# A two-layer hybrid backbone on one core: router with stationary weights, one expert unit split by GpSimd, streamed end, later mod trips, stationary V

## What is computed

```python
# Layer l:  h = RMSNorm(x) * (1 + scale1) + shift1      (shift/scale/gate = SiLU(c) W_mod + b_mod)
#           P = h W_in  -> [q | k | v | hyena v,x1,x2 | gate_a | gate_b]
#           x += gate1 * ((sigmoid(gate_a) * A W_pa + sigmoid(gate_b) * Bh W_pb) W_o)
#           x += gate2 * FFN(RMSNorm(x) * (1 + scale2) + shift2)
def channel_mixer(h, l, ffn_w1, ffn_w3, ffn_w2, moe_router, moe_w1, moe_w3, moe_w2):
    i = l // 2
    if l % 2 == 0:
        return swiglu(h, ffn_w1[i], ffn_w3[i], ffn_w2[i])
    logits = (h @ moe_router[i]).astype(jnp.float32)
    top_val, top_idx = lax.top_k(logits, TOP_K)
    gate = jax.nn.softmax(top_val, axis=-1)
    ...
    for e in range(N_EXPERTS):
        out = out + weight[..., e:e + 1] * swiglu(h, moe_w1[i, e], moe_w3[i, e], moe_w2[i, e])
    return out
```

## Time and profile before

| | |
|---|---|
| median of 3 runs | 2063.52 us (2061.28 to 2065.64) |
| the profiled execution | 2065.47 us |
| its span in the trace | 2063.4 us |
| PE busy | 1956.9 us, 95% of the span |
| DVE busy | 1237.7 us, 60% |
| ACT busy | 999.3 us, 48% |
| GpSimd busy | 49.2 us, 2% |
| transferred | 435.46 MB, mean 211 GB/s |

### The profile page before, as it was taken

How to read it: one execution, slowest core, us unless ns; L and a number is a source line. 1 busy time by engine, 2 the same in 40 slices (tenths; PEclk the granted TensorE clock), 3 DMA queues, 4 the chain that set the end, 5 groups by cost and what they waited for, 6 DMA issues and landing times. The chain is left out here.

```text
span 2063.4 us, 24969 instructions
## 1 busy us (share of the span) xinstructions
PE 1956.9 (95%) x10036; PEld 1574.4 (76%) x10036; DVE 1237.7 (60%) x1194; ACT 999.3 (48%) x931; POOL 49.2 (2%) x57
## 2 busy tenths in 40 slices
PE   8999999998999989999998969999999999999995
PEld 3677777786888867768877967888888888888884
DVE  3444545445323322246544557897989798979894
ACT  4221145433433421134135437676777677767772
POOL 0000000002000001100000000000000000000000
PEclk9999999999999999999999969999999999999998
DMA  9641211133222246633222437897989799989991
GB/s 369 263 171 41 86 41 62 62 113 114 84 99 102 95 175 278 243 113 123 96 72 89 147 146 296 336 383 297 387 338 387 290 382 350 371 310 371 351 364 43
DMA packets 63109, 435.46 MB, mean 211 GB/s; under 512 B 7008, under 2 KB 8160, under 8 KB 13344
## 3 DMA queue, kind: packets, MB, share of 16 engines
q1 hardware_dynamic: 58112, 400.88, 50.8%
q0 software_dynamic: 4896, 33.13, 4.1%
HBM read 432.94 MB, written 1.05 MB: 210 GB/s over the span
## 5 line engine op out<-in xcount | busy, mean ns | idle before, releaser
L1243 DVE TENSOR_TENSOR expert_lo<-expert_raw,expert_hi 128x2048 fp32r<-128x2048 f32 x264 | 598.7, 2288 | 88.0 <-ACT expert_hi L767 87.9
L767 ACT ACTIVATE expert_hi<-expert_raw 128x2048 fp32r<-128x2048 f32 x264 | 504.2, 1917 | 123.6 <-PE psum L1827 69.8
L524 ACT ACTIVATE units_hi<-raw_units 128x2048 fp32r<-128x2048 f32 (+2 forms) x88 | 147.3, 1673 | 524.0 <-PE psum L1358 441.9
L1356 PE MATMUL psum<-h_hi,units_hi 128*128 128x512 f32 (+1 forms) x928 | 348.3, 375 | 18.2 <-DVE h_lo L938 8.9
L892 DVE TENSOR_TENSOR units_lo<-raw_units,units_hi 128x2048 fp32r<-128x2048 f32 (+2 forms) x88 | 175.2, 1991 | 315.1 <-ACT units_hi L524 315.1
L1358 PE MATMUL psum<-h_hi,units_lo 128*128 128x512 f32 (+1 forms) x928 | 335.3, 361 | 0.0
L1357 PE MATMUL psum<-h_lo,units_hi 128*128 128x512 f32 (+1 forms) x928 | 335.1, 361 | 0.0
L1825 PE MATMUL psum<-expert_hi,gathered_hi_lo 128*128 128x512 f32 (+1 forms) x768 | 291.4, 379 | 3.5 <-DVE expert_lo L1243 2.4
L1827 PE MATMUL psum<-expert_hi,gathered_hi_lo 128*128 128x512 f32 (+1 forms) x768 | 286.5, 373 | 0.0
L1826 PE MATMUL psum<-expert_lo,gathered_hi_lo 128*128 128x512 f32 (+1 forms) x768 | 286.4, 373 | 0.0
L1356 PEld LDWEIGHTS psum<-h_hi,units_hi 128*128 128x128 f32 x928 | 175.8, 189 | 64.2 <-issue 33.3
(11 more groups left out here) (256 smaller groups left out, 2533.7 us busy)
## 6 DMA issues: line engine op xcount, KB each, us to landing
expert_raw<-in_moe_w SPq DMA_DIRECT2D x264, 1024.0 KB, 6.2
raw_units<-in_w_in SPq DMA_DIRECT2D x40, 1024.0 KB, 4.8
mod_units<-in_w_mod POOLq DMA_DIRECT2D x24, 1024.0 KB, 10.6
raw_units<-in_ffn_w SPq DMA_DIRECT2D x22, 1024.0 KB, 4.7
raw_units<-in_ffn_w SPq DMA_DIRECT2D x16, 704.0 KB, 4.2
raw_units<-in_w_pab SPq DMA_DIRECT2D x16, 512.0 KB, 3.5
raw_units<-in_w_o SPq DMA_DIRECT2D x8, 1024.0 KB, 4.7
mod_units_a<-in_w_mod SPq DMA_DIRECT2D x5, 1024.0 KB, 4.8
```

The costliest lines, as they stand in the source:

```text
L767: A(EH[:, SPLIT_AT[j], :], eraw[:, RAW_AT[j], :], ACT.Copy).then_inc(e_hi, 1)
L1243: TT(EL[:, s, :], eraw[:, RAW_AT[j], :], EH[:, s, :].bitcast(F32), ALU.subtract).then_inc(e_lo, 1)
L1356: MM(o, wh, xh, start=first, stop=False)
```

## The change

It has five parts.

- **Mod trips.** `mod_units` of a block m now stands behind s = 1, and `mod_turn` of block m - 1 behind s = 0 of block m. On DVE `mod_row` and `mod_out` of block m - 1 both stand behind the `lo` of the unit that replaces s = 0 of block m.
- **Attention.** V is now the stationary operand: two heads at a time, each in its own half of the array's columns (64 wide), with the probabilities of 128 queries moving. The result is already turned, so `heads_turn` is gone; in its place the reciprocal sums are spread to 64 columns a head and transposed (`sums_turn`), and DVE multiplies by them after a copy.
- **Router.** The 8 router columns are the stationary operand and a slice's 256 tokens move: three matmuls a slice, each slice followed by its two transposes to token order. The logits are then turned back by two small matmuls. On DVE the gates' arithmetic is moved behind the first expert units' work (`gate_weights`), and the first two gathers' copies ahead of it.
- **GpSimd.** Unit 28 of the first expert is rounded and split by GpSimd (a copy, a subtraction) and no longer by ACT and DVE.
- **End.** For the last expert unit 30 goes to split slot 3, last used by unit 23, and is rounded and split in the step of unit 26 (`END_AT`), and the middle's last transposes stand ahead of unit 27; the scatter, the residual's update and the norm's squares stand behind the `If` and run slice by slice.

The core of the diff:

```diff
+            pool.wait_ge(n_pe, 8 * 3 + pooled[3])
+            for n, j in enumerate(BY_POOL):
+                pool.wait_ge(e_in[RAW_AT[j]], 16 * first_loads_of(0, j))
+                pool.wait_ge(e_use, place_of(0, -1, before(j, SPLIT_AT)))
+                nc.gpsimd.tensor_copy(EH[:, SPLIT_AT[j], :], eraw[:, RAW_AT[j], :]).then_inc(p_hi, 1)
+                pool.wait_ge(p_hi, n + 1)
+                pool.wait_ge(e_lo, place_of(0, -1, j - 1))
+                nc.gpsimd.tensor_tensor(EL[:, SPLIT_AT[j], :], eraw[:, RAW_AT[j], :], EH[:, SPLIT_AT[j], :].bitcast(F32),
+                                        ALU.subtract).then_inc(e_lo, 1)
...
                 def ehi(e, j, n):
+                    end = j == LAST_DOWN and isinstance(e, int) and e == NE - 1
                     act.wait_ge(e_in[RAW_AT[j]], 16 * n)
-                    act.wait_ge(e_use, place_of(g, e, before(j, SPLIT_AT)))
-                    A(EH[:, SPLIT_AT[j], :], eraw[:, RAW_AT[j], :], ACT.Copy).then_inc(e_hi, 1)
+                    act.wait_ge(e_use, place_of(g, e, END_BEFORE if end else before(j, SPLIT_AT)))
+                    A(EH[:, END_SLOT if end else SPLIT_AT[j], :], eraw[:, RAW_AT[j], :], ACT.Copy).then_inc(e_hi, 1)
...
+                    if m >= 2 and m - 2 < len(steps) and steps[m - 2][1] == HEADS - 1:
+                        n = att_n + m - 2
+                        dve.wait_ge(a_ex, n + 1)
+                        r0 = (n + 1 - HEADS) % 32
+                        link(V_.reciprocal(rsum[:, r0:r0 + HEADS], psums[:, r0:r0 + HEADS]))
+                        V_.tensor_copy(rs[:].rearrange("p (h d) -> p h d", h=HEADS),
+                                       rsum[:, r0:r0 + HEADS].unsqueeze(2).to_broadcast([P, HEADS, HD])).then_inc(a_rb, 1)
+                    if m >= 3 and m - 3 < len(steps) and steps[m - 3][1] == HEADS - 1:
+                        dve.wait_ge(a_o, (att_n + m - 2) // 2)
+                        link(V_.tensor_copy(ON[:], PS[:, 7, :]))
+                        dve.wait_ge(a_ot, att_q + 1)
+                        TT(ON[:], ON[:], PS[:, 6, :], ALU.mult).then_inc(a_on, 1)
...
                         lo(b["down"] + 2 * m + 2, 0, 11 * P if m < DK - 1 else 2048)
-                        if m < MTRIPS:
-                            mod_row(1, m)
+                        if 1 <= m <= MTRIPS:
+                            mod_row(1, m - 1)
+                            mod_out(1, m - 1)
...
                         lo(b["down"] + 2 * m + 3, 1, 11 * P if m < DK - 1 else 2048)
-                        if m < MTRIPS:
-                            mod_out(1, m)
...
+            V_.tensor_copy(logits_t[0:NE, :], PS[0:NE, 4, 0:L]).then_inc(r_lt, 1)
+            tokens_lo(0)
+            dve.wait_ge(bias_in, 16 * 6)
+            dve.wait_ge(r_pe, 2)
...
+                link(V_.tensor_copy(tif[:, c, :], ti[:, c, :]))
+                TS(oh[:, c, 0, :], iot[:, 0:NE], tif[:, c, 0:1], None, ALU.is_equal)
+                link(TS(oh[:, c, 1, :], iot[:, 0:NE], tif[:, c, 1:2], None, ALU.is_equal))
+                TT(msk[:, c, :], oh[:, c, 0, :], oh[:, c, 1, :], ALU.add).then_inc(r_mask, 1)
...
+            def gate_weights():
+                for c in range(2):
+                    dve.wait_ge(r_ev, c + 1)
+                    link(TS(gt[:, c, 2:3], gt[:, c, 1:2], 1.0, None, ALU.add))
+                    link(V_.reciprocal(gt[:, c, 2:3], gt[:, c, 2:3]))
...
+                    if last and j == END_AT:
+                        dve.wait_ge(e_lo, place_of(g, e, NEXT0 - 1))
+                        dve.sem_inc(e_lo, 2)
+                        elo(e, LAST_DOWN)
...
-                    pe.wait_ge(a_pt, n + 1)
+                    pe.wait_ge(a_pt, n + 2)
                     if h == 0:
-                        pe.wait_ge(a_on, att_q + (m > 0))
+                        pe.wait_ge(a_on, att_q)
                     nk = 4 if qc >= 2 else 2
                     for kc in range(nk):
-                        last = MM(PS[:, 7, h * HD:(h + 1) * HD], PT[:, n % 2, kc * P:(kc + 1) * P],
-                                  V[:, kc, h * HD:(h + 1) * HD], start=kc == 0, stop=kc == nk - 1)
+                        for j in range(2):
+                            last = MM(PS[j * HD:(j + 1) * HD, 7, h * HD:h * HD + P], V[:, kc, (h + j) * HD:(h + j + 1) * HD],
+                                      PTS[n // 2 % 2][:, j, kc * P:(kc + 1) * P], start=kc == 0, stop=kc == nk - 1)
                     last.then_inc(a_o, 1)
 
...
-                def heads_turn(qc, turned):
-                    pe.wait_ge(a_on, att_q + 1)
+                def sums_turn(turned):
+
+                    pe.wait_ge(a_rb, att_q + 1)
                     pe.wait_ge(a_pt, att_n + turned)
                     for c in range(4):
-                        last = TR(PS[:, 6, c * P:(c + 1) * P], OT[:, qc % 2, c * P:(c + 1) * P], ident)
+                        last = TR(PS[:, 6, c * P:(c + 1) * P], rs[:, c * P:(c + 1) * P], ident)
                     last.then_inc(a_ot, 1)
 
...
                                 norm_sums(2, [m - 1])
-                            if s == 0 and m < MTRIPS:
-                                mod_units(1, m)
+                            if s == 0 and 1 <= m <= MTRIPS:
+                                mod_turn(1, m - 1)
                         if m < MTRIPS:
-                            mod_turn(1, m)
+                            mod_units(1, m)
...
+                MM(PS[0:NE, 4, 0:L], RTH[:, k, :], RH[:, k, :], start=k == 0, stop=False)
+                MM(PS[0:NE, 4, 0:L], RTH[:, k, :], RL[:, k, :], start=False, stop=False)
+                last = MM(PS[0:NE, 4, 0:L], RTL[:, k, :], RH[:, k, :], start=False, stop=k == DK - 1)
+                if k == DK - 1:
+                    last.then_inc(r_pe, 1)
...
-                    last = MM(o, RH[:, k, x_], RTL[:, k, :], start=False, stop=k == DK - 1)
+                    turned = TR(PS[:, HTB[2 * (k // 4) + c], k % 4 * P:(k % 4 + 1) * P], mo_h[:, k, c * P:(c + 1) * P], ident)
...
                         if j == NEXT0:
                             turn_mid(e, UPS - 1)
+                        if last and j == NEXT0 - 1:
+                            turn_mid(e, UPS - 1)
                         if last and j == LAST_DOWN:
-                            turn_mid(e, UPS - 1)
...
+            pe.wait_ge(e_yl, NE + 1)
+            for r in range(4):
+                scatter_slice((0, 1, 5, 6)[r], r).then_inc(f_sc, 1)
```

165 lines of the change are left out of this document (92 added, 73 removed).

## The result

The changed kernel takes 2069.48 us (median of 8 runs, 2065.75 to 2075.0), the kernel before 2062.96 (8 runs beside them, 2061.05 to 2065.64). The ratio is 1.003, with a 95% interval of 1.0019 to 1.0041: slower by 0.3%. Foretold were 2064.5, with 2052 to 2077 for the range, so the time lies in the range and 5.0 us above the forecast.

What follows compares the result with a forecast made beforehand. PE was taken as the bound, with only its own work, standstills and half clock to win. Mod trips +17.5, attention -7.5, router +3 and end -12 sum to +1.0: 2066.5 profiled, 2064.5 on the median's scale, range 2052 to 2077.

Steps and rivals of the forecast that it cites:

- Mod trips: Layer 0's down stage: six added waits and half clock outweigh the first trip's savings; +17.5 us, ends +8 and +22.
- The chain from s = 0 to the copy: Down stage: ACT's rounding 1.38, DVE's lo 1.63 and row copy 0.42 hold PE's transposes 3.7 to 3.95 us.
- The rival of a dearer clock: Down stage's six waits: two half-clock stretches behind each, 3.4 us and not 1.5; +11.4, time 2076; chance 0.16.
- the free one: Down stage: the clock stays full behind the six waits, all else as forecast; -9, time 2055.5; chance 0.08.
- Attention: Both layers' attention: PE work and waits saved, DVE's copy and product added at the ends; -7.5 us, from -11 to +3.
- The pair's cost of 1.24: Latent block's product with V: two heads on overlapping column halves cost 1.24 us of PE's sequence, saving 0.56.
- the wait that "goes": Layer 0's attention: of 2.4 us that transposes wait for the output's low half, 1.95 is won.
- Router and first unit: Router to first up units: -3.6 without GpSimd, +6.5 for GpSimd holding DVE at the norm; +3 us, from -6 to +6.
- The end: From the last down unit to the norm's root: earlier unit and slice-by-slice sums; -12 us, from -10 to -14.
- The term for unit 30's own slot: Last down unit: no 4.60 us wait and twelve matmuls in 2.7, so it ends 6.4 us earlier.
- 0.7 (the `If`): The end: passing the conditional ahead of the streamed residual, squares and sums was to take 0.7 us.
- The sign: Whole kernel, bounds 2059.4 and 2067.6: faster 0.28, within 0.37, slower 0.35.

Runs made afterwards that it cites:

- mod_only: The kernel before with only the mod trips' part of the change, on PE and DVE: 2082.75 us, ratio 1.0091.
- after: The changed kernel itself, with all five parts, against the kernel before: 2069.48 us, ratio 1.003.
- pool_late: Changed kernel with the mod transposes behind s = 1, and GpSimd starting unit 28 only once the router norm's slices are made: 2043.39 us, ratio 0.9894.
- no_second: Changed kernel with the mod transposes behind s = 1, and the never-entered conditional second round of experts left out: 2037.53 us, ratio 0.986.

## Why the prediction was right, point by point

- **The bound** (PE's waits and half clock, not other engines' work) held: all that moved is PE's own work (attention), its waits or its clock.
- **Mod trips**, +17.5: measured +16.9. The chain from s = 0 to the copy was right to a few tenths, waits of 3.52 against 3.7 to 3.95 and 2.66 against 3.2, 20.3 against 22.3. The clock cost 9.2 where 9 was taken, though not as foretold, 1.5 at each of six waits: 2.8 at the first, about 1.6 at each of the next four, nothing at the last. What is left, 12.6, was won where 13.3 was taken. The rival of a dearer clock (3.4 a wait) did not come, though the first wait did bring two stretches; nor did the free one, since five of six waits were followed by half clock.
- **Attention**, -7.5: measured -4.7. The pair's cost of 1.24 was right and with it nearly the 5.2 of PE's work (3.9 of time and 1.0 of added waits make 4.9). The step that failed is the wait that "goes": of the 2.4 us at the block ends of layer 0 1.7 went, where 1.95 was taken. In their place came 1.8 us of waits for scores and probabilities, which the sum didn't have, and 0.8 at the layer's end, where it had 1.2. In layer 1 the 2.37 went, waits of 1.34 and longer ones for ACT (2.17, where 1.60 stood) came, and the forecast's 1.5 for that layer isn't shown at all: `mod_only`, with the old product and the same wait of 2.37, has no half clock behind it, and its stage is as short as the changed kernel's.
- **Router and first unit**, +3: measured -0.4. The sum hid two errors. GpSimd held DVE as forecast, 5.1 us at the slices where 6.5 was taken, and 7.7 to 10 over the whole way to the first down unit, which falls to 1.1 once the gates stand elsewhere. The router without it was worth 7.2 to 9.5 and not 3.6: I had priced each change of the array's division at 0.15 to 0.25 and a slice at 1.4 to 1.6; a slice took 1.07 at half clock, so the changes cost nothing there. No run has the new router without the moved gates and gathers' copies, so the 7.2 to 9.5 are not divided between them.
- **The end**, -12: measured -7.5. The term for unit 30's own slot (6.4) measured 5.9. The term that failed is the stream: "0.7 (the `If`)" stood for 2.3 us behind the operands' wait and 2.5 more inside the scatter. The root came 15.5 us after the last down unit's end, not 12. The trace of before had shown the same 4.98 ahead of the sums, and I read it as ACT's squares alone.
- **The scale**: 2064.5 was 5.0 too low. The parts make 2.8 of it (2069.27 for the profiled execution after, 2066.5 foretold). The rest is the 1.95 that I took off because the profiled execution of before lay above its median; the one after lay 0.2 under its own. That the parts come so near is in part luck: they were off by -0.6 (mod trips), +2.8 (attention), -3.4 (router), +4.5 (the end) and -0.4 (the rest).
- **The sign**: with +1.0 as the sum, no change was likeliest (0.37) and slower next (0.35); it became slower.

## What to carry to other kernels

An instruction that waits should stand on its engine behind the work that covers the wait, and the cover is a matter of order: the same transposes lost 17 us in one place and, half a block later, let the trip's 8 to 10 be won. Work given to an idle engine has a price where it shares a port with the engine that sets the end; it is to be priced at the busy engine's instructions beside it, not at its own, and again after each change to that engine's queue (7.7 to 10 us here, 1.1 once the gates stood elsewhere). And before work is streamed behind a conditional, look in the trace for what stands behind that conditional already.

## What the runs showed of the hardware

- GpSimd held DVE where it began first. Its subtraction (4.75 us) held a two-input DVE instruction of 0.48 for 4.2 us (`after`), another (4.49) a 128 x 8 conversion of 0.17 for 3.6 (`pool_late`), and its copy of 1.89 a two-input subtraction of 0.23 for 1.5 (`after`). The DVE instruction that began 0.09 ahead of GpSimd's was not held; nor, in `pool_late`, were a maximum and an index search on 128 x 8 beside the subtraction, or DVE instructions with one PSUM and one SBUF input beside the copy.
- Passing over a conditional body that isn't entered, with the loading of its flag, cost PE some 4.5 us in two pieces, the second behind the fourth of sixteen matmuls, and the end 5.5 us in all (`no_second` against the changed kernel). In the nine profiles that have both the round and the stream, the second piece is 1.8 to 2.5.
- Waits of 3.52 us brought 3.4 us of half clock four times and 6.8 once; the one of 2.66 none. The wait of 2.37 in layer 1 had 3.4 us of half clock behind it in the kernel before and none in `mod_only`.
